# Attention outputs go unnormalised into the output projection, and the root of the norm is multiplied in at each eviction

## The reference, cut to what matters

```
y   = xf * rsqrt(mean(xf * xf, axis=-1) + EPS)        # rmsnorm, then y * g
mix = concatenate([rmsnorm(out_a, na_out_g), rmsnorm(out_b, mla_out_g)], axis=-1)
h   = h + mix @ w_out
h   = h + conv_glu(rmsnorm(h, ffn_norm_g), w_gate, w_up, conv_w, conv_b, w_down)
```

## Time and profile before

| | us |
|---|---|
| median of 3 runs | 2760.75 |
| lowest, highest | 2756.81, 2762.22 |
| the profiled execution | 2758.96 |
| its span | 2757.6 |
| PE busy | 2676.1 (97%) |
| DVE busy | 1830.9 (66%) |
| ACT busy | 1244.6 (45%) |
| POOL busy | 341.9 (12%) |

### The profile page before, as it was taken

One profiled execution on the slowest core, in us unless ns is written; L12 is line 12 of the kernel. 1 busy time (PEld: TensorE's weight loads), 2 busy tenths in 40 slices (PEclk: granted clock), 3 DMA queues, 4 the chain that ended last, 5 costly groups with the idle time before them and its releaser, 6 DMA issues.

```text
span 2757.6 us, 51315 instructions
## 1 busy us (share of the span) xinstructions
PE 2676.1 (97%) x22036; PEld 2633.7 (96%) x22036; DVE 1830.9 (66%) x2554; ACT 1244.6 (45%) x1935; POOL 341.9 (12%) x550
## 2 busy tenths in 40 slices
PE   6999999899999999998999999999989999999998
PEld 6888889899999999998999999999989999999998
DVE  6666568777777777776788667766854445454444
ACT  4556554544433444445444443334544433344443
POOL 3110113111111111231000001110210000000001
PEclk9999999999999999999999999999999999999999
DMA  6433357588888888885444578886745555655553
GB/s 192 139 108 104 116 181 234 194 273 268 267 282 282 274 268 267 270 279 179 154 153 144 179 234 269 271 277 215 255 153 192 190 174 189 193 193 185 182 183 125
DMA packets 500083, 571.20 MB, mean 207 GB/s; under 512 B 26704, under 2 KB 473424, under 8 KB 499856
## 3 DMA queue, kind: packets, MB, share of 16 engines
q1 hardware_dynamic: 467968, 463.76, 51.8%
q0 software_dynamic: 31600, 103.80, 11.9%
q10 hardware_dynamic: 288, 0.36, 0.0%
HBM read 565.77 MB, written 2.54 MB: 206 GB/s over the span
## 4 chain that ended last, share of the span: by engine, by line
PE 85%; DVE 8%; ACT 4%; issue 2%; DMA 1%; POOL 0%; DVEq 0%; SPq 0%; ACTq 0%
PE ps L672 27%; PE ps L673 26%; PE ps L674 26%; DVE wl L1764 2%; ACT wh L1274 2%; PE ps L952 1%; PE ps L798 1%; DVE nx L1856 1%; DVE ada_acc L1983 1%; DVE lr L1930 1%; DVE sqt L1856 0%; DMA raw<-in_w_in 0%; ACT lp L1442 0%; PE ps L639 0%; PE ps L823 0%
## 5 line engine op out<-in xcount | busy, mean ns | idle before, releaser
L1764 DVE TENSOR_TENSOR wl<-raw,wh 128x1024 fp32r<-128x1024 f32 (+1 forms) x894 | 1056.4, 1198 | 639.6 <-ACT wh L1274 635.3
L672 PE MATMUL ps<-xx,wh 128*128 128x256 f32 (+2 forms) x4848 | 1385.6, 286 | 30.9 <-DVE xx L1839 15.1
L673 PE MATMUL ps<-xx,wh 128*128 128x256 f32 (+2 forms) x4848 | 1364.9, 282 | 0.0
L674 PE MATMUL ps<-xx,wl 128*128 128x256 f32 (+2 forms) x4848 | 1362.2, 281 | 0.0
L1274 ACT ACTIVATE wh<-raw 128x1024 fp32r<-128x1024 f32 (+1 forms) x894 | 881.8, 1029 | 618.8 <-PE ps L674 601.2
L672 PEld LDWEIGHTS ps<-xx,wh 128*128 128x128 f32 x4848 | 916.4, 189 | 42.2 <-DVE xx L1839 12.3
L673 PEld LDWEIGHTS ps<-xx,wh 128*128 128x128 f32 x4848 | 917.5, 189 | 1.7 <-issue 1.0
L674 PEld LDWEIGHTS ps<-xx,wl 128*128 128x128 f32 x4848 | 917.0, 189 | 0.0
L672 PE MATMUL ps<-hid,wh 128*128 128x256 f32 x1408 | 393.9, 280 | 0.0
L673 PE MATMUL ps<-hid,wh 128*128 128x256 f32 x1408 | 393.7, 280 | 0.0
L674 PE MATMUL ps<-hid,wl 128*128 128x256 f32 x1408 | 392.8, 279 | 0.0
(11 more groups left out here) (362 smaller groups left out, 2400.8 us busy)
## 6 DMA issues: line engine op xcount, KB each, us to landing
raw<-in_w_in SPq DMA_DIRECT2D x118, 1024.0 KB, 5.3
ada_raw<-in_w_ada POOLq DMA_DIRECT2D x384, 256.0 KB, 4.7
raw<-in_w_gate SPq DMA_DIRECT2D x44, 1024.0 KB, 6.3
raw<-in_w_up SPq DMA_DIRECT2D x44, 1024.0 KB, 6.7
raw<-in_w_ffn_gate SPq DMA_DIRECT2D x44, 1024.0 KB, 5.1
raw<-in_w_ffn_up SPq DMA_DIRECT2D x44, 1024.0 KB, 5.1
raw<-in_w_down SPq DMA_DIRECT2D x32, 1024.0 KB, 6.2
raw<-in_w_ffn_down SPq DMA_DIRECT2D x32, 1024.0 KB, 5.4
```

What stands on the lines that cost most here:

```text
L672: pe.matmul(dst, h[:, c, o:o + w], x[:, 0, k, g.t0:g.t1], start=(k == 0), stop=False)
L673: pe.matmul(dst, h[:, c, o:o + w], x[:, 1, k, g.t0:g.t1], start=False, stop=False)
L674: m = pe.matmul(dst, l[:, c, o:o + w], x[:, 0, k, g.t0:g.t1], start=False, stop=end)
L1764: dve.tensor_tensor(wl[i % NS][:, part], raw[i % NR][:, part], wh[i % NS][:, part].bitcast(F32), ALU.subtract).then_inc(s_lo, 1)
```

## The change

The chunks of `out_b` and `out_a` are no longer multiplied by `rstd`. `finish` on ScalarE makes the high half of value times norm weight (activation with a per-partition scale), `finish` on VectorE the low half in one instruction from the head's output; GpSimd has no part in it any more. The squares are summed and the root and its reciprocal are taken beside or after that, the root of `out_b` in `ssq["b"]`, that of `out_a` in `rstd`. On every engine the program waits ahead of `outb` and `outa` only for the head lanes, and drains `fin_b` and `fin_a` after the first product of each. Each eviction of `outb` and `outa` becomes two instructions on VectorE: bank times root into a scratch tile (`scaled_out`, which frees the bank), and that tile plus the residual.

```diff
+NORM_SCALED = [16, 4, 2, 0, 0, 16, 16, 16]
...
+        def root_of(n):
+            return ssq["b"] if n == N_B else rstd
+
+        def heads_base(n):
+            return 0 if n == N_B else 8
...
# TensorE
                 yield from pause(2)
                 square_sums(n)
-                yield
-                yield
-                yield
...
-            lanes.drain("fin_b")
+            def heads_ready(n):
+                def ready(k):
+                    pe.wait_ge(s_al, heads_base(n) + k + 1)
+                return ready
+
+            lanes.drain("mla0", "mla1")
             lanes.start("ada", ada(), slow=True)
             for g in range(8):
-                gemm(("outb", g), normed(N_B) if g == 0 else None)
-            lanes.drain("fin_a")
+                gemm(("outb", g), heads_ready(N_B) if g == 0 else None)
+                if g == 0:
+                    lanes.drain("fin_b")
+            lanes.drain("na0", "na1")
             for g in range(8):
-                gemm(("outa", g), normed(N_A) if g == 0 else None)
+                gemm(("outa", g), heads_ready(N_A) if g == 0 else None)
+                if g == 0:
+                    lanes.drain("fin_a")
...
# GpSimd: finish() is gone
-            lanes.drain("fin_b")
+            lanes.drain("mla0", "mla1")
...
             pool.dma_start(h2[:, :, :], hT[:, 0:8, :]).then_inc(s_h2[0], 16)
-            pool.wait_ge(s_nlv, NORM_HALF[N_B + 1])
-            pool.wait_ge(s_nlp, NORM_HALF[N_B + 1])
+            pool.wait_ge(s_al, 8)
             pool.dma_start(H[:, 8:16, :], hT[:, 8:16, :]).then_inc(s_h2[1], 16)
...
# ScalarE
             def finish(n, slab_done, *after):
                 while lanes.running(*after):
                     yield
-                yield from pause(2)
+                act.wait_ge(s_slab, slab_done)
+                for i in range(8):
+                    act.activation(NORM_DST[n][:, 0, i, Q0:T], norm_src(n, i), ACT.Copy, scale=norm_gain(n, i)).then_inc(s_ah, 1)
+                    if i % 4 == 3:
+                        yield
+                yield
                 root(n)
-                yield
-                yield from norm_his(n, slab_done)
...
-                    squares(N_FFN1, 2 * g + j, H[:, 2 * g + j, 14:T], *last_use(("outa", g), j))
+                    squares(N_FFN1, 2 * g + j, H[:, 2 * g + j, 14:T], s_ob, 16 + 2 * g + j + 1)
...
# VectorE
-                yield from pause(2)
+                yield
+                for i in range(8):
+                    h = NORM_DST[n][:, 0, i, Q0:T]
+                    dve.wait_ge(s_ah, heads_base(n) + i + 1)
+                    dve.scalar_tensor_tensor(out=NORM_DST[n][:, 1, i, Q0:T], in0=norm_src(n, i), scalar=norm_gain(n, i), in1=h.bitcast(F32),
+                                             op0=ALU.mult, op1=ALU.subtract).then_inc(s_al, 1)
+                    if i % 4 == 3:
+                        yield
+                yield
                 reciprocal(n)
-                yield
-                yield from norm_scales(n)
+
+            def scaled_out(key, j, n, i):
+                s, _ = last_use(key, j)
+                x = (nx[0], nx[1] if n == N_B else ssq["b"])[j][:, 0:T - Q0]
+                if i >= 2:
+                    dve.wait_ge(s_ob, i - 1)
+                dve.tensor_tensor(x, ps[GEMMS[key].banks[j]][:, 0:T - Q0], root_of(n)[:, 0:T - Q0], ALU.mult).then_inc(s, 1)
+                dve.wait_ge(*last_use(key, j))
+                return x
...
             for g in range(8):
                 gemm(("outb", g))
+                if g == 0:
+                    lanes.drain("fin_b")
                 dve.wait_ge(s_slab, done(("outb", g)))
+                dve.wait_ge(s_rr, N_B + 1)
                 for j in range(2):
                     c = 2 * g + j
-                    s, _ = last_use(("outb", g), j)
                     dve.wait_ge(s_h2[0 if c < 8 else 1], 16)
                     old = h2[:, c, 14:T] if c < 8 else H[:, c, 14:T]
-                    dve.tensor_tensor(old, ps[GEMMS[("outb", g)].banks[j]][:, 0:T - 14], old, ALU.add).then_inc(s, 1)
+                    x = scaled_out(("outb", g), j, N_B, c)
+                    dve.tensor_tensor(old, x, old, ALU.add).then_inc(s_ob, 1)
...
                 for j in range(2):
                     c = 2 * g + j
-                    dve.wait_ge(*last_use(("outb", g), j))
-                    residual(("outa", g), j, c, 14, old=h2[:, c, 14:T] if c < 8 else None)
+                    dve.wait_ge(s_ob, 16 if c < 2 else 16 + c - 1)
+                    x = scaled_out(("outa", g), j, N_A, 16 + c)
+                    old = h2[:, c, 14:T] if c < 8 else H[:, c, 14:T]
+                    dve.tensor_tensor(H[:, c, 14:T], x, old, ALU.add).then_inc(s_ob, 1)
```

More of the change, by code:

```diff
@@ L272 @@
 NORM_SHIFT = [False, False, False, False, False, False, True, True]
-NORM_X = [sum(NORM_CHUNKS[:n]) for n in range(9)]
-NORM_HALF = [sum(NORM_CHUNKS[:n]) // 2 for n in range(9)]
+NORM_SCALED = [16, 4, 2, 0, 0, 16, 16, 16]
+NORM_X = [sum(NORM_SCALED[:n]) for n in range(9)]
+NORM_HALF = [sum(NORM_SCALED[:n]) // 2 for n in range(9)]
 NORM_Y = [sum(c // 2 for c, s in zip(NORM_CHUNKS[:n], NORM_SHIFT) if s) for n in range(9)]
@@ L523, in build @@
         s_shh, s_shl = sem("shift_hi"), sem("shift_lo")
+        s_ah, s_al, s_ob = sem("heads_raw_hi"), sem("heads_raw_lo"), sem("out_scaled")
         s_sv, s_gs, s_fs = sem("shift_kept"), sem("first_gate_scaled"), sem("first_forget_sigmoid")
@@ L1079, in latent @@
                 yield from norm_lows(N_CKV)
-            def finish(n, *after):
-                while lanes.running(*after):
-                    yield
-                yield from pause(2)
-                yield
-                yield from norm_lows(n)
             def attend():
@@ L1174, in gpsimd_program @@
                     lanes.start("mla0", mla(0, p), front=True)
-                    if p == 3:
-                        lanes.start("fin_b", finish(N_B, "mla0", "mla1"))
                     continue
@@ L1182, in gpsimd_program @@
                     lanes.start("na0", na(0, p), front=True)
-            lanes.start("fin_a", finish(N_A, "na0", "na1"))
-            lanes.drain("fin_b")
+            lanes.drain("mla0", "mla1")
             hT = A["hT"].rearrange("(c p) t -> p c t", p=P)
@@ L1350, in root @@
                     act.wait_ge(s_nx, NORM_X[n])
-                act.activation(rstd[:, 0:m], PX[2][:, 0:m], ACT.Sqrt, bias=eps, scale=1.0 / (NORM_D[n] if n < 8 else D)).then_inc(s_rs, 1)
+                act.activation(root_of(n)[:, 0:m], PX[2][:, 0:m], ACT.Sqrt, bias=eps, scale=1.0 / (NORM_D[n] if n < 8 else D)).then_inc(s_rs, 1)
             def norm_his(n, slab_done):
@@ L1824, in reciprocal @@
                 dve.wait_ge(s_rs, n + 1)
-                dve.reciprocal(rstd[:, 0:m], rstd[:, 0:m]).then_inc(s_rr, 1)
+                x = root_of(n)[:, 0:m]
+                dve.reciprocal(x, x).then_inc(s_rr, 1)
             def norm_scales(n):
@@ L2085, in vector_program @@
                 gemm(("outb", g))
+                if g == 0:
+                    lanes.drain("fin_b")
                 dve.wait_ge(s_slab, done(("outb", g)))
+                dve.wait_ge(s_rr, N_B + 1)
                 for j in range(2):
                     c = 2 * g + j
-                    s, _ = last_use(("outb", g), j)
                     dve.wait_ge(s_h2[0 if c < 8 else 1], 16)
                     old = h2[:, c, 14:T] if c < 8 else H[:, c, 14:T]
-                    dve.tensor_tensor(old, ps[GEMMS[("outb", g)].banks[j]][:, 0:T - 14], old, ALU.add).then_inc(s, 1)
+                    x = scaled_out(("outb", g), j, N_B, c)
+                    dve.tensor_tensor(old, x, old, ALU.add).then_inc(s_ob, 1)
                 if g == 2:
                     bounds()
-            lanes.drain("fin_a")
+            lanes.drain("na0", "na1")
             for g in range(8):
                 gemm(("outa", g))
+                if g == 0:
+                    lanes.drain("fin_a")
+                    dve.wait_ge(s_al, 16)
+                    dve.wait_ge(s_sq["a"], 8)
+                    dve.wait_ge(s_rr, N_A + 1)
                 dve.wait_ge(s_slab, done(("outa", g)))
[L2099 to L2102, removed]
                 for j in range(2):
                     c = 2 * g + j
-                    dve.wait_ge(*last_use(("outb", g), j))
-                    residual(("outa", g), j, c, 14, old=h2[:, c, 14:T] if c < 8 else None)
+                    dve.wait_ge(s_ob, 16 if c < 2 else 16 + c - 1)
+                    x = scaled_out(("outa", g), j, N_A, 16 + c)
+                    old = h2[:, c, 14:T] if c < 8 else H[:, c, 14:T]
+                    dve.tensor_tensor(H[:, c, 14:T], x, old, ALU.add).then_inc(s_ob, 1)
                 raw_lows(N_FFN1, RAW_LAG[N_FFN1].get(g, []))
```

3 lines of the change are left out of this document (removed).

## The result

The changed kernel takes 2767.86 us, the median of nine runs (2761.87 to 2768.48), against 2759.74 for nine runs of the kernel before beside it. The recorded ratio of the runs is 1.002, with a 95% interval of 1.0011 to 1.0028: **slower by 5.5 us (3.0 to 7.7)**, at the edge of what was called no change. The two medians alone lie 8.1 us apart; the text goes by the ratio and its interval. The profiled execution is 2765.75 us with a span of 2764.4 (before: 2758.96 and 2757.6).

A forecast was written before the change was run, and what follows sets the result against it. VectorE's queue was taken as the bound: 112.6 + 1.7 + 14.4 - 5.9 + 3.2 - 3.2 - 2.8 = 120.0 us from 367.1 ends at 487.1 against 487.07, so no difference: 2760.8 us, range 2753.5 to 2765.5.

The forecast's parts named there:

- the half clock: Rival: after waits TensorE's clock halves near the heads' last products and feed-forward, delaying VectorE's queue; +6.3, 2767.1 us, chance 0.10.
- VectorE's queue: From 374 to 527 us VectorE's work sets the time, 6.6 us per `outa` product; no difference, chance 0.60.
- TensorE's view: Rival: VectorE is not the limit, so TensorE gains standstill, slow clock and bank wait; -6.7, 2754.1 us, chance 0.13.
- Start of the queue: VectorE's first weight low behind the norm of `out_b` starts at 367.1 instead of 374.5, 7.4 us earlier.
- Evictions: Each of 16 products of `outb` and `outa` takes 1.57 instead of 0.67 us on VectorE, +14.4 in all.
- its rival of -3.7: Rival: the evictions' multiply and wait cost only 0.67 us a product; 2757.1 us, chance 0.12.
- Weight wait over `out_a`: VectorE idles 2.8 us for the weight high behind the second head's output in ScalarE's queue; 4.13 before.
- The other two waits: VectorE's waits of 1.11 and 0.77 us for root and high halves over the norm of `out_a` go.
- Weight loads: VectorE's waits of 1.38 and 1.44, traced to ScalarE's 7.60 wait for a slab, go; -2.8 us, ends 0 and -2.8.
- GpSimd's masks: Bias masks behind GpSimd's wait before the second load are wanted 10 us later; no cost entered.
- my window: VectorE's queue from its first weight low behind the norm of `out_b` to the feed-forward operands' last low halves; 112.6 us before.
- TensorE's new waits: TensorE, ahead in `outa`, waits about 1.9 us for `ada`, 1.4 and 1.7 for banks, 2.6 at the sum of squares.

The follow-up runs named there:

- no_mul: Changed kernel without the multiply by the root at the evictions of `outb` and `outa`; 2753.61 us, ratio 0.9969 to the kernel before.
- the free pair: Changed kernel and kernel before, both with early bias masks, late `ada` start and some `ada` steps doubled up; 2749.87 and 2755.06 us.
- before_late_ada: Kernel before with the `ada` lane started behind `outa` instead of ahead of `outb`; 2760.31 us, ratio 0.9993 to the kernel before.
- masks_early: Changed kernel with GpSimd's last two bias masks added before the product ('na', 3, 2); 2763.33 us, ratio 1.0008 to the kernel before.
- after_late_ada: Changed kernel with the `ada` lane started behind `outa` instead of ahead of `outb`; 2756.56 us, ratio 0.9981 to the kernel before.
- outb_only: Changed kernel with the change undone for `out_a`, so only `outb` keeps it; 2762.75 us, ratio 1.0001 to the kernel before.
- after_free: Changed kernel with early bias masks, late `ada` start and some `ada` steps doubled up; 2749.87 us, ratio 0.9956 to the kernel before.
- outb_only_free: Change for `outb` alone, plus early bias masks, late `ada` start and doubled-up `ada` steps; 2753.50 us, ratio 0.9971 to the kernel before.
- before_free: Kernel before with early bias masks, late `ada` start and some `ada` steps doubled up; 2755.06 us, ratio 0.9975 to the kernel before.

## Why the prediction was right, and where its sum was off

The time of 2760.8 with no change was forecast, in a range of 2753.5 to 2765.5, and the runs give +0.20% (0.11 to 0.28). The kernel before timed beside it plus 5.5 is 2765.2, just inside the range; the median of 2767.86 by itself is 2.4 us above it, and the interval leaves out a difference of nothing. So the mechanism held, and the sum was too low by 3.6 us of the stage: the width of the range took that in. (Its upper end is called half way to the half clock; half way would be 2764.0.) Point by point:

- **The bound is VectorE's queue, TensorE's view is wrong: confirmed.** The 2.62 us of standstill and the slow clock behind it are gone (0.12 pitch, clock 1.00 at 368 to 370), and nothing is gained; no_mul and the free pair gain as soon as that queue has room.
- **Start of the queue:** predicted 367.1, measured 368.39 - 1.58 (upstream) = 366.8.
- **Evictions:** 0.90 us a product predicted, 0.92 measured in `outa` (7.5 against 6.6, pairs of 0.45), 14.5 us for all 16 instead of 14.4. The rule by which the wait would be free, and its rival of -3.7, fall.
- **Weight wait over `out_a`:** 2.8 predicted, 3.19 measured. The other two waits of the earlier trace rows are gone.
- **Weight loads, the first term that failed.** I took both waits of 1.38 and 1.44 off, as the work of one slab that landed late. The 1.38 is gone, the 1.44 is there again (439.52), and in every other kernel here too. ScalarE's timeline shows why, first before, then after: its two weight halves stand behind the squares of `outa`'s first eviction, which themselves wait for VectorE. That was no DMA, and nothing of the change moves it.

```profile
438.92 0.42 ACT L1391 ACTIVATE ssq_h<-H 128x258 f32<-128x258 f32 x1 [3.14 <-DVE H L2014]
...
439.58 1.99 ACT L1274 ACTIVATE wh<-raw 128x1024 fp32r<-128x1024 f32 x2
```
```profile
437.32 0.42 ACT L1394 ACTIVATE ssq_h<-H 128x258 f32<-128x258 f32 x1 [6.78 <-DVE H L2138]
...
438.44 2.00 ACT L1277 ACTIVATE wh<-raw 128x1024 fp32r<-128x1024 f32 x2
```

- **GpSimd's masks, the larger one.** "Its bias masks behind it are wanted 10 us later" asked only when their result is needed, and costed them at nothing. They stretch the weight low beside them from 1.23 to 4.26: +3.0. It is the term that failed by most. The masks stood at the same time in the kernel before, and did the same there, inside the norm of `out_b`. Its timelines of GpSimd and of VectorE:

```profile
369.01 2.88 POOL L1117 TENSOR_TENSOR na_bias<-na_bias,cst 128x512 f32<-128x512 f32 x2
```
```profile
367.06 1.15 DVE L1856 SCALAR_TENSOR_TENSOR nx<-out_b,vec,rstd 128x258 f32<-128x258 f32 x2
...
368.58 2.18 DVE L1856 SCALAR_TENSOR_TENSOR nx<-out_b,vec,rstd 128x258 f32<-128x258 f32 x2
370.69 1.49 DVE L1839 TENSOR_TENSOR xb<-nx,xb 128x258 fp32r<-128x258 f32 x1
```

  That was readable beforehand: two steps that take 1.15 just ahead of the masks take 2.18 beside them, and a low half of 0.42 takes 1.49. Since it lay ahead of the queue's first weight low, my window did not hold it; the change pulled the window's start over it.
- **The sum:** 120.0 + 3.0 (masks) + 1.4 (weight load) + 0.4 (wait at `out_a`) + 0.1 (evictions) = 124.9. Against it 0.8 of small waits around the softmaxes falls away; that is 124.1 of the measured 124.0. The raw low halves take no part: their rows are shorter (1.27 against 1.38 a pair), but from their start to the next weight low it is 1.35 in both kernels (468.14 to 469.49, 465.58 to 466.93). Of the 4.0 us too many, 0.3 come back at the start: +3.7.
- **TensorE's new waits:** `ada` 1.9 predicted and 3.3 measured; the bank 1.4 and 1.7 predicted near 467 and 475, one of 1.5 measured at 481.94, ahead of the feed-forward's first product; the sum of squares 2.6 and 1.2. All three kinds came.
- **The sum of squares before the change, a row that was read wrong.** The prediction takes the 0.6 us of the earlier trace rows for a wait of TensorE at the feed-forward's first product. It is a row of the whole span, and the wait stands at 2744.97, at the end of the second block. At the feed-forward's sum there was no wait before:

```profile
484.67 0.70 PE L736 MATMUL ps<-sqt,cst 128*128 128x258 f32 x2
...
2744.97 0.70 PE L736 MATMUL ps<-sqt,cst 128*128 128x256 f32 x2 [0.59 <-ACT sqt L1395]
```

  So this row does not show where VectorE's queue reaches TensorE in the kernel before. What shows that it does is before_late_ada, whose stage is 5.6 us shorter with two steps a product fewer on VectorE; TensorE's own wait and transposes for `ada` can be 1.6 of that at most (0.9 and 0.7 in its expectation).
- **Half clock:** not seen on the queue. The clock was 1.00 at 395 to 405; it fell to 0.74 at 446 to 452, around the 3.3 of `ada`, where TensorE was ahead and the queue went on. That the runs came out on this rival's side is in the larger part the masks' work, as masks_early shows.

What stays open: between the stage's +3.6 and the runs' +5.5 lie 1.9 us. In the two profiles the part behind the stage is 1.5 us longer after the change (2255.9 and 2257.4), 0.8 of it ahead of ScalarE's next table load (1141.79 before). Whether that is scatter or comes from the waits of the feed-forward is not shown.

## What to carry to other kernels

When work moves off the engine that waits and onto the one that sets the pace, sum the pace-setter's own queue; the removed wait of 2.6 us was worth nothing until that queue had room, and then the same edit was worth 5.2 us of runs and 3.5 of the stage. A window for such a sum must begin ahead of the earliest point to which the change can pull its start, and an operation of another engine is costed at nothing only after looking at how long its neighbours take beside it. Ask of every wait that you strike whether its releaser was itself waiting for the engine you are summing.

## What the runs showed of the hardware

**GpSimd against VectorE.** A VectorE subtraction with both inputs in SBUF took 4.26 us beside two GpSimd additions of 2.52 together. It took 4.25 to 4.27 in the three other kernels where the additions stand beside it (no_mul, after_late_ada, outb_only), and 1.23 in the three where they don't (masks_early, after_free, outb_only_free). The Trainium skill has the rule, which I had not weighed ("SBUF — State Buffer", section "SBUF: two separate sides"): the two engines share a pair of ports as an exclusive lock for whole instructions, and the loser is blocked, where VectorE has two SBUF inputs and GpSimd reads SBUF too. The size roughly agrees, 3.03 lost against 2.52 held: the subtraction ends 1.10 us behind the additions (372.65 and 371.55), nearly its whole length. The order doesn't: the Trainium skill gives the ports to whichever starts first, and by the records VectorE's instruction began 0.64 us ahead of the masks and was still the one that was stretched (spans on GpSimd are rough).

**The clock after a wait.** The same wait of 2.62 us at the same place was followed by a granted clock of 0.50 in the kernel before, and of 1.00 in before_free, whose matmul and window are these:

```profile
370.30 0.36 PE L676 MATMUL ps<-xb,wh 128*128 128x258 f32 x1 [2.62 <-DVE xb L1854]
```
```profile
370.00:372.00 2.00, 1.67 (x12) 1.49 (x12) 1.93 (x5) 1.29 (x5) 1.18 (x2) 1.00 0.02 4
```

In before_late_ada, with the same wait ahead of 369.38, the clock was 1.00 from 370 to 372 too, and 0.50 only from 374.5 to 377.9. So the length of that wait alone doesn't decide it, and a fall read from one profile is not a sure term of a sum.
